# Product-key experts: one gather for four slots of 32 tokens, V summed through 32-column weights

## The reference, cut to what matters

```python
idx = jnp.take_along_axis(...)            # 8 heads x 16 best of 16384 experts per token
gate = jax.nn.softmax(best_s, axis=-1)
act = jax.nn.gelu(jnp.einsum('thkd,td->thk', u_tab[idx], hb), approximate=False)
return jnp.einsum('thk,thkd->td', gate * act, v_tab[idx])
```

## Time and profile before

| | us |
|---|---|
| median of three runs | 5071.84 (5067.22 to 5077.32) |
| the profiled execution | 5067.13 |
| its span, first to last instruction | 5065.3 |
| PE busy in the span | 3905.9 (77%) |
| DVE busy | 3247.4 (64%) |
| POOL busy | 1442.1 (28%) |
| ACT busy | 743.5 (15%) |
| TensorE clock granted, mean | 0.918 of full speed |

### The profile page before, as it was taken

One profiled execution on the slowest core, in us unless ns is written; L12 is line 12 of the kernel. 1 busy time (PEld: TensorE's weight loads), 2 busy tenths in 40 slices (PEclk: granted clock), 3 DMA queues, 4 the chain that ended last, 5 costly groups with the idle time before them and its releaser, 6 DMA issues. The chain is left out here.

```text
span 5065.3 us, 36421 instructions
## 1 busy us (share of the span) xinstructions
PE 3905.9 (77%) x11046; PEld 1925.4 (38%) x11046; DVE 3247.4 (64%) x8263; ACT 743.5 (15%) x2205; POOL 1442.1 (28%) x1284
## 2 busy tenths in 40 slices
PE   7479577889777777778868776789987777777776
PEld 6365233554223222235535632346432322222222
DVE  1534866644887867854474648664468787687666
ACT  0121124311101001010022111341111100100101
POOL 0001122211444444432222011222134444344432
PEclk9689688999998999999989887899999999999999
DMA  8244346763998998999959334567469999899998
GB/s 262 71 131 142 140 174 225 260 220 128 404 418 362 421 421 365 421 395 390 371 205 355 135 125 159 205 237 259 156 252 421 388 401 421 366 421 421 415 421 343
DMA packets 342149, 1497.72 MB, mean 296 GB/s; under 512 B 31424, under 2 KB 176448, under 8 KB 178112
## 3 DMA queue, kind: packets, MB, share of 16 engines
q0 software_dynamic: 184320, 1342.26, 66.2%
q1 hardware_dynamic: 157632, 153.13, 9.4%
HBM read 1491.97 MB, written 3.31 MB: 295 GB/s over the span
## 5 line engine op out<-in xcount | busy, mean ns | idle before, releaser
L650 PE MATMUL expert_acc<-uv_ring,diag 128*128 128x512 f32 x3744 | 1895.4, 640 | 430.1 <-DVE diag L1207 420.7
L604 POOL DMA_INDIRECT uv_ring<-uv,expert_index x936 | 1051.9, 1124 | 2816.8 <-PE expert_acc L650 2249.1
L650 PEld LDWEIGHTS expert_acc<-uv_ring,diag 128*128 128x128 f32 x3744 | 702.1, 201 | 1515.1 <-DVE diag L1207 898.2
L1198 DVE CUSTOM_DVE_ANT_0 uv_ring<-uv_ring,arena 128x1024 f32<-128x1024 f32 x680 | 832.0, 1224 | 236.9 <-DMA uv_ring<-uv,expert_index 234.1
L650 PE MATMUL expert_acc<-arena,diag 128*128 128x512 f32 x1376 | 692.4, 636 | 258.1 <-DVE diag L1207 189.8
L1207 DVE TENSOR_SCALAR diag<-const_mats,expert_gate,gelu 128x128 f32<-128x128 f32 x1280 | 465.4, 364 | 372.9 <-ACT gelu L929 276.4
L929 ACT ACTIVATE gelu<-u_dot 128x1 f32<-128x1 f32 x1280 | 256.3, 203 | 2995.9 <-DVE u_dot L1198 2991.9
L604 POOL DMA_INDIRECT arena<-uv,expert_index x344 | 390.0, 1134 | 763.6 <-PE expert_acc L650 465.2
L1198 DVE CUSTOM_DVE_ANT_0 arena<-arena 128x1024 f32<-128x1024 f32 x344 | 420.9, 1224 | 174.1 <-DMA arena<-uv,expert_index 172.4
L650 PEld LDWEIGHTS expert_acc<-arena,diag 128*128 128x128 f32 x1376 | 248.6, 197 | 692.9 <-DVE diag L1207 403.4
L1198 DVE CUSTOM_DVE_ANT_0 uv_ring<-uv_ring,prompt_rows 128x1024 f32<-128x1024 f32 x256 | 312.2, 1220 | 86.8 <-DMA uv_ring<-uv,expert_index 86.1
(11 more groups left out here) (201 smaller groups left out, 2788.3 us busy)
## 6 DMA issues: line engine op xcount, KB each, us to landing
w_ring<-w_ada SPq DMA_DIRECT2D x66, 512.0 KB
w_ring<-w_in SPq DMA_DIRECT2D x64, 512.0 KB
w_ring<-w_pq SPq DMA_DIRECT2D x64, 512.0 KB
w_ring<-w_out SPq DMA_DIRECT2D x32, 512.0 KB
uv_ring<-w_ada SPq DMA_DIRECT2D x30, 512.0 KB, 6.0
uv_ring<-uv,expert_index POOLq DMA_INDIRECT x936
arena<-b_ada SPq DMA_DIRECT2D x48, 128.0 KB
arena<-uv,expert_index POOLq DMA_INDIRECT x344
```

Source lines behind the costliest of these rows:

```text
L604: pool.indirect_dma_start(out=UV[j], out_offset=None, in_=uv, in_offset=bass.IndirectOffsetOnAxis(ap=idxs[:, n % 2, k:k + 1], axis=0)).the ...
L650: ins = pe.matmul(acc[:, half, :], diag[:, m % DIAGS, :], UV[SLOT_AT[m]][:, D + 512 * half:D + 512 * half + 512], start=(k == 0), stop=(k ...
L1198: V_.tensor_tensor_reduce(UV[j][:, 0:D], UV[j][:, 0:D], rows_of(n), 1.0, 0.0, ALU.mult, ALU.add, dots[:, m % DOTS:m % DOTS + 1]).then_inc( ...
```

## The change

A gather now brings, for one quarter q of the tokens (32 of them, `QUAD`), four slots at once: partition 32s + t holds token 32q + t in slot 4k + s. There are still 128 gathers a block of the same 128 rows. The weights of a gather are then 128x32, the same 32-column diagonal pattern (`same`) in each quarter of the partitions, and the sum over partitions adds the four slots. The result of half 0 goes to PSUM partitions 32q to 32q + 31, that of half 1 to the quarter two further on, so `add_peer` adds the second half crosswise. Gathers run through (k, q) in the diagonal order `STEPS`: quarter 0 begins first and ends first (at steps 118, 122, 125 and 127 the quarters end).

Token rows must stand four times: `spread_rows` makes eight tiles of 16 matmuls (weights 128x32 of hT, identity moving) in place of two tiles of four transposes, and ACT copies them into `rows4`, which there is once. For the first block of a group it stands after the scores; for block b + 1, six tiles stand on PE behind `add_v` of step 110 and two behind step 127. The ring has 4 buffers instead of 5 (alone: 6, 7, 8 and 8 instead of 7, 8, 9 and 9), the weight matrices of `weigh` have 8 instead of 4 buffers. Indices and gates are written by 16 instructions of 32 partitions instead of one. The tables of points are the same.

```diff
-RING, SPARE = 5, 4
-DIAGS, DOTS = 4, 16
+RING, SPARE = 4, 4
+DIAGS, DOTS = 8, 16
+QUAD = P // 4
+STEPS = sorted(((k, q) for k in range(SLOTS // 4) for q in range(4)), key=lambda t: (t[0] + t[1], t[1]))
+SPREAD_AT = 110
...
                 pe.wait_ge(s_dg, m + 1)
+                four, q = STEPS[k]
                 for half in range(2):
-                    ins = pe.matmul(acc[:, half, :], diag[:, m % DIAGS, :], UV[SLOT_AT[m]][:, D + 512 * half:D + 512 * half + 512],
-                                    start=(k == 0), stop=(k == SLOTS - 1), skip_group_check=True)
+                    at_ = QUAD * ((q + 2 * half) % 4)
+                    ins = pe.matmul(acc[at_:at_ + QUAD, half, :], diag[:, m % DIAGS, :],
+                                    UV[SLOT_AT[m]][:, D + 512 * half:D + 512 * half + 512],
+                                    start=(four == 0), stop=(four == SLOTS // 4 - 1), skip_group_check=True)
...
+                    def spread_rows(b, first=0, last=8):
+                        for i in range(first, last):
+                            t = fill("ht", l, g, 8 * b + i)
+                            lo = b * P + QUAD * (i // 2)
+                            for c in range(4):
+                                for s in range(4):
+                                    ins = pe.matmul(t[QUAD * s:QUAD * s + QUAD, c * P:(c + 1) * P], hT[:, 4 * (i % 2) + c, lo:lo + QUAD],
+                                                    C[:, C_ID, :], start=True, stop=True)
+                            done(ins, "ht")
...
                     score_block(0, 2, 4)
                     beside.rest()
+                    spread_rows(0)
...
                             add_v(n, k)
+                            if b + 1 < nb and k == SPREAD_AT:
+                                spread_rows(b + 1, 0, 6)
+                        if b + 1 < nb:
+                            spread_rows(b + 1, 6, 8)
...
+                    def drain_rows(b, q, l=l, g=g):
+                        n = blk(l, g, b)
+                        if n:
+                            act.wait_ge(s_dot, (n - 1) * SLOTS + LAST_OF[q] + 1)
+                        if n and q == 3 and b == 0:
+                            act.wait_ge(s_pup.sem, n)
+                        for half in range(2):
+                            t = tile_of("ht", l, g, 8 * b + 2 * q + half)
+                            nc.scalar.activation(rows4[:, q, 512 * half:512 * half + 512], t, ACT.Copy).then_inc(free["ht"].sem, 1)
...
-                V_.tensor_tensor_reduce(UV[j][:, 0:D], UV[j][:, 0:D], rows_of(n), 1.0, 0.0, ALU.mult, ALU.add,
+                V_.tensor_tensor_reduce(UV[j][:, 0:D], UV[j][:, 0:D], rows4[:, q, :], 1.0, 0.0, ALU.mult, ALU.add,
...
-                V_.tensor_scalar(diag[:, m % DIAGS, :], C[:, C_ID, :], gat[:, n % 2, k:k + 1], gel[:, m % DOTS:m % DOTS + 1],
+                V_.tensor_scalar(diag[:, m % DIAGS, :], same[:], gat[:, n % 2, q, four:four + 1], gel[:, m % DOTS:m % DOTS + 1],
...
+                for k in range(2):
+                    ins = V_.tensor_tensor(tmp[64 * k:64 * k + 64], acc[64 - 64 * k:128 - 64 * k, 1, :], gate[64 - 64 * k:128 - 64 * k, 512:D], ALU.mult)
...
+                        for q in range(4):
+                            of = slice(QUAD * q, QUAD * q + QUAD)
+                            for s in range(4):
+                                ins = V_.tensor_tensor(idxs[QUAD * s:QUAD * s + QUAD, blk(l, g, b) % 2, q, fours], pick4[of, 0, fours, s],
+                                                       pick4[of, 1, fours, s], ALU.add)
```

More of the change, by code:

```diff
@@ L50 @@
 SLOTS = PH * TOPK
-RING, SPARE = 5, 4
-DIAGS, DOTS = 4, 16
+RING, SPARE = 4, 4
+DIAGS, DOTS = 8, 16
+QUAD = P // 4
+STEPS = sorted(((k, q) for k in range(SLOTS // 4) for q in range(4)), key=lambda t: (t[0] + t[1], t[1]))
+LAST_OF = {q: STEPS.index((SLOTS // 4 - 1, q)) for q in range(4)}
+SPREAD_AT = 110
 WU = 256
 NW = 3
-AHEAD = 5
-ARENA = 16392
+AHEAD = 6
+ARENA = 15636
 ADA_UNITS = 6 * D // WU
@@ L237, in psum_order @@
             out += [("n2", l, g, i) for i in range(2 * nb)]
-            out += [("pq", l, g, i) for i in range(8)] + [(s, l, g, i) for s in ("ht", "ps") for i in range(2)]
+            out += [("pq", l, g, i) for i in range(8)] + [("ps", l, g, 0), ("ps", l, g, 1)]
             out += [("pq", l, g, i) for i in range(8, 16)] + [("ps", l, g, 2), ("ps", l, g, 3)]
+            out += [("ht", l, g, i) for i in range(8)]
             for b in range(1, nb):
-                out += [("ht", l, g, 2 * b), ("ht", l, g, 2 * b + 1)]
                 out += [("ps", l, g, 4 * b + i) for i in range(4)]
+                out += [("ht", l, g, 8 * b + i) for i in range(8)]
     return out
@@ L279, in build @@
         G = sb("gates", [P, 5, D])
-        C = sb("const_mats", [P, 7, P])
+        C = sb("const_mats", [P, 6, P])
+        iota16 = sb("iota", [P, TOPK])
+        same = sb("same_token", [P, QUAD])
         rp = sb("rope_tables", [P, 4, 2, ROPE])
@@ L858, in _ @@
                     pe.wait_ge(*free["n2"].at(l, g, 2 * nb - 1))
-                    def score_block(b, first=0, last=4):
-                        for half in range(0 if first else 2):
-                            t = fill("ht", l, g, 2 * b + half)
-                            for c in range(4):
-                                ins = turn(t[:, c * P:(c + 1) * P], hT[:, 4 * half + c, b * P:(b + 1) * P])
-                            done(ins, "ht")
+                    def spread_rows(b, first=0, last=8):
[7 more added lines that the diff above has]
+                            done(ins, "ht")
+                    def score_block(b, first=0, last=4):
                         for k in range(first, last):
@@ L1098, in drain_scores @@
                     def drain_scores(b, first=0, last=4):
-                        for half in range(0 if first else 2):
-                            t = tile_of("ht", l, g, 2 * b + half)
-                            if b >= 2 and half == 0:
-                                act.wait_ge(s_dot, (blk(l, g, b) - 1) * SLOTS)
-                            nc.scalar.activation((htok[b % 2] if g else htok_p[:])[:, 512 * half:512 * half + 512], t, ACT.Copy).then_inc(free["ht"].sem, 1)
                         for k in range(first, last):
@@ L1231, in _ @@
             beside = Beside(dot_beside)
-            dve.wait_ge(s_const.sem, 16 * 7)
+            dve.wait_ge(s_const.sem, 16 * 8)
             dve.wait_ge(s_x.sem, 16)
+            for q in range(4):
+                ins = V_.tensor_copy(same[QUAD * q:QUAD * q + QUAD, :], C[QUAD * q:QUAD * q + QUAD, C_ID, QUAD * q:QUAD * q + QUAD])
+            chain(ins)
             for l in range(L):
@@ L1242, in _ @@
                 if l:
-                    dve.wait_ge(*full["ht"].at(l - 1, 1, 7))
+                    dve.wait_ge(*full["ht"].at(l - 1, 1, 31))
                 dve.wait_ge(*s_condt.at(l))
```

72 lines of the change are left out of this document (40 added, 32 removed), and 2 rows, old and new, of the table FULL_COUNTS.

## The result

The changed kernel takes 5243.36 us (median of 4 runs, 5239.49 to 5247.51) against 5071.03 us (4 runs, 5067.22 to 5077.32): ratio 1.0339, 95% interval 1.0321 to 1.0357. It is 172 us slower. The prediction said 31 slower on the profiled execution and gave 5095 in all, 23 above the kernel before. The sign and the range (4970 to 5250) held; the size did not.

A forecast was written before the change was run, and what follows sets the result against it. It took DMA to bound seven of ten blocks, with PE's chain longest in the sample mixers' projections. Its terms -136 + 51 + 13 + 12 + 8 + 73 + 10 = +31 on 5067.1 made 5098, given as 5095; range 4970 to 5250.

The forecast's parts named there:

- the change's own work: Token rows four times +51, step 110 +13, transitions between blocks +12, other index and gate writes with `add_peer` +8.
- V sums: Sums over slots on PE shorten from 1.72 to 0.86 us each, mostly beside the sample mixers: -136 us together.
- clock: Shorter sums leave PE idler, so some mixer matmuls fall to the lower clock level: +10 us (0 to 40).
- four of the first ones: Four single-slot points of the first projections in each sample block, counted among 30 points gaining 0.86 us each.
- close pairs in the first projection: Part of the missing buffer's cost, in each sample block's first projection: 4 us of 29 a block.
- Ring: One buffer less beside the mixers makes third gathers late at three-slot points: +73 us (20 to 110).
- Pairs: Rival, 62%: sums overlap in pairs at 0.86 us a slot, costs and gains near each other; range 5020 to 5170.
- four groups: Rival, 18%: all four column groups run at once, a sum takes 0.43 us, kernel faster at 4985 us.
- no overlap: Rival, 17%: products queue whatever their weight columns, so sums gain nothing: +295 us, 5360.
- Mode changes: Switching between 128- and 32-column weights at every point: 0; a 3% rival had 0.26 us a change, 5164 in all.
- Step 110 and transitions: Six row tiles at step 110 idle DMA with 6 buffers: +13 us; gathers waiting between blocks: +12.
- the prediction's first sign of being wrong: The prediction is wrong if the alone stages no longer run at 421 GB/s with 6 buffers.

The follow-up runs named there:

- e1: Kernel before with four slot buffers instead of five beside the mixers, one fewer too in the alone stages: 5281.5 us, ratio 1.0405.
- e2: Kernel before with every sum of V over 256 instead of 512 columns a record, slot 0 excepted: 5026.96 us, ratio 0.9910.
- e13: Kernel before with four slot buffers and 256-column sums together: 5148.89 us, ratio 1.0147.
- e5: Changed kernel with its fifth buffer back, paid for by two weight tiles instead of three: 5154.48 us, ratio 1.0143.
- e9: Changed kernel with two slots of 64 tokens a gather instead of four of 32, and a fifth buffer: 5039.86 us, ratio 0.9936.
- e4: Changed kernel with each row tile made by 4 plain transposes instead of 16 products: 5222.61 us, ratio 1.0284.
- e14: Changed kernel with one write of the indices and four of the gates instead of 16 each: 5179.29 us, ratio 1.0209.
- e8: Changed kernel with both products of a slot in the same column group: 5381.34 us, ratio 1.0598.
- e12: e9 with useless zero-weight products behind the sums of the prompt stage alone: 5021.95 us, ratio 0.9899.
- e10: e2 with useless zero-weight products behind the sums of the heads and prompt stage: 5004.95 us, ratio 0.9866.

## Why the prediction was right in its sign and wrong in its size

The four corners, and the changed kernel beside them, in us against the kernel before:

```
                        five buffers      four buffers
long sums                    0             +205 (e1)
short sums                 -46 (e2)         +75 (e13)
the change's own work                      +172 (changed kernel), so +97 above e13
```

- **V sums and clock: forecast -136 and +10, measured -46** with five buffers. This is the step that failed worst. (18 of the 136 were for a shorter `weigh`, which e2 leaves as it is: in the changed kernel it is 36 ns shorter, not 160, and what that gives is in the third corner.) Sized right were the points where PE sets the pace: output projection -12.8 a block (forecast 13.8), query projection -14.6 (forecast 13). Wrong were the heads, counted at -15 a block, measured +6.6 and +7.5, and the prompt stage, counted at -10, measured +20.7. The prediction named the clock and put +10 on it from windows of the convolution; it did not ask what happens in stretches where PE was at 0.96 to 0.99 only because the long sums filled it. In the prompt stage the lower clock is the cause as far as the fillers show: with filler the loss goes from 20.7 to 2.5 us. In the heads a filler gives 3 of the 22 us a block that are missing, with the clock at 0.92; the heads are still 4 us longer than before. So the sums there were not on the path, and shortening them could not gain 15. What else lengthens them by 4 us stays open. The "four of the first ones", and the "close pairs in the first projection" of the ring's sum, were no points of sums at all: the choice's 14 steps run there.
- **Ring: forecast +73, measured +121** beside short sums (+205 beside long ones). The forecast looked only at points with three slots. It had the scan steps at +18 a block; in e13 against e2 slots 16 to 32 lose 7 and 32 to 48 win 2, because DVE's wait for the transfer stands in place of one that it had there anyway (2.69 us ahead of the decay product L1420 before, 0.64 or less at the same place, L1456, in the changed kernel, and nothing to 0.52 in e13). With long sums the same steps do lose: 24 and 27 us a block (e1, slots 30 to 54). The heads, with one and two slots a point and not in the sum, lose 17.5 and 22.7 a block (e13 against e2), the points just ahead of them (slots 48 to 60: two scan steps and two other points of three slots) 14, where some 9 was forecast. The prompt stage loses 22.6 instead of 15, and the alone stages 11 by slots instead of nothing. The mechanism was the forecast's own: a gather goes out only when PE has summed an earlier slot, and takes 5.7 us to its use. It was not carried to the heads: 24 points in 146 us (slots 60 to 96) are 6.1 us each, and a gather that goes out only behind a sum has little of that left. That the wait is there and goes with the fifth buffer is shown (e1, e5, e9); this count of microseconds is an argument.
- **The change's own work: forecast 51 + 13 + 12 + 8 = +84, measured +97**: nearly right in sum, wrong in its parts. The 97 is a difference of two corners, so the sum below closes by construction; it also holds what the output and query projections lose against e13, some 20 us by slots, where the mode changes below are. The row products were too dear (0.9 us a tile, not 1.9; e4: 28 in all, with the stall at 110 at 2.9 us instead of 6.5 a layer). The old tiles were misread on top: the 1.04 us of the earlier trace rows is for both tiles of a block, so 4, not 9, was to be taken off. The index and gate writes were far too cheap: 66 (e14) where the forecast had 8 and, of the 12 for the transitions, the gates' share. There are 576 writes in place of 36, most of them of these forms:

```profile
L1670 DVE TENSOR_TENSOR expert_index<-arena 32x16 uint32<-32x16 f32 x256 | 45.3, 177 | 3.8
...
L1687 DVE TENSOR_TENSOR expert_gate<-arena 32x16 f32<-32x16 f32 x256 | 43.8, 171 | 3.8
```

  A quarter of the partitions takes 171 ns, as 128 partitions do with the same 16 columns. All 576 are 102 us of DVE, hidden only where DVE has slack.
- **Overlap.** Pairs was right for a lone slot (0.98 us against 0.86 forecast), four groups for neighbouring slots (1.00 us for two), so the first two rivals were both true in their places, and the row tiles went by the second (7 us for eight); no overlap is excluded. The 18% rival had its time wrong all the same, because the gain was not in the sums' length any more.
- **Mode changes: forecast 0, measured 0.16 us each.** The 16 products ahead of a sum take 3.66 us to its start (1050.37 to 1054.03) against 3.45, and the sum 0.98 to the next product against 0.86 in e2: 0.21 and 0.12, together 0.33 a point with its two changes. It is the same where nothing overlaps (e8: 3.65 and 1.84 against 3.45 and 1.72). The output projection gains 8.0 us by slots in the changed kernel and 12.8 in e2; 16 points of 0.33 are 5.3 of it. The rival priced it at 0.26 a change; the mechanism is there, and the row without a gap did not exclude it. The Trainium skill (TensorEngine Tiling (Array Packing), Key Properties) says that a change of mode drains the engine; the traces agree that a change costs, 0.16 us here, and do not show whether the engine is drained.
- **Step 110 and transitions.** The stall of six tiles showed with six buffers (+2.9) and not with seven (0), as the prediction had it. The transitions lose 7.6, 5.9 and 3.4 us in layer 0 (from slot 112 to the next block's first); in each of the six blocks with another behind them 5.3 to 5.4 us fall at step 122, with the gate writes, and 0.4 in e14. The stretches without such a place still run at 421 GB/s (4600 to 4700), but over the alone stages it is 395 and 399 instead of 403 and 406: the prediction's first sign of being wrong shows in part.

With these the sum is -46 + 121 + 97 = 172, against -126 + 73 + 84 = 31. The order matters: on four buffers short sums are worth 130 (e1 to e13; e8 against the changed kernel says 131), since the gathers then wait for PE's sums. The prediction summed both on the kernel before.

## What to carry to other kernels

Price a prefetch buffer by running one less before a change takes it away: here the fifth of five was worth 121 to 205 us, more than the matmul saving that it paid for (46 with five buffers, 130 with four). Work taken off TensorE gains only where TensorE sets the pace; elsewhere it can lower the granted clock, and the products around it become slower (381 to 425 ns in the modulation). Splitting partitions cost an instruction per part at full price on VectorE here (171 ns each), so take the smallest split that gives the overlap: two groups of 64 did here what four of 32 did, with a quarter of the writes and half of the rows, and e12 is 1.0% faster than the kernel before where the change was 3.4% slower.

## What was not expected of the hardware

- Products of float32 with 512 moving columns in four column groups run at once: 8 records in 1.00 us, against 1.72 us for 4 in one group. The Trainium skill (TensorE: Matmul & The Clock Gate, section Packing small matmuls) gives 2.38 times for three groups; here four gave 3.4 times (3.44 / 1.00).
- Going between 128-column weights and 32- or 64-column ones costs 0.16 us a change with the stream full, as the mean of both ways (e9, 64 columns: 3.65 and 1.01 us, as with 32).
- A kernel got faster by useless matmuls: 22 us in e10 against e2 and 18 us in e12 against e9 (18.2 and 12.4 of it by slots in the prompt stage), with the granted clock of the modulation at 0.97 to 0.99 instead of 0.86 to 0.88.
